# A two-block transformer kernel on one core: finer first tiles, an unsplit out-projection, and a reordered VectorE queue

## The reference, cut to what matters

```
mod = split(silu(c) @ ada_w + ada_b, 6)                  # ada_w: 1024 x 6144, one row vector c
a   = rmsnorm(x, g_pre) * (1 + mod[1]) + mod[0]
b_gate, c_gate, v = split(a @ sc_w_in, 3)                # 1024 x 3072
y   = (b_gate * depthwise_conv3(c_gate * v)) @ sc_w_out  # 1024 x 1024
x   = x + mod[2] * rmsnorm(y, g_post)
h   = rmsnorm(x, g_pre_ff) * (1 + mod[4]) + mod[3]
x   = x + mod[5] * rmsnorm(relu(h @ mlp_w_in)**2 @ mlp_w_out, g_post_ff)
```

## Time and profile before

| what | us |
|---|---|
| runs | 793.24 median of three (791.18 to 793.31) |
| profiled execution, its time | 792.01 |
| its span, first to last instruction | 790.2 |
| PE busy | 754.2 (95%) |
| DVE busy | 554.6 (70%) |
| ACT busy | 370.2 (47%) |
| moved by DMA | 152.17 MB, 193 GB/s |

### The profile page before, as it was taken

How to read it: one execution, slowest core, us unless ns; L and a number is a source line. 1 busy time by engine, 2 the same in 40 slices (tenths; PEclk the granted TensorE clock), 3 DMA queues, 4 the chain that set the end, 5 groups by cost and what they waited for, 6 DMA issues and landing times.

```text
span 790.2 us, 13306 instructions
## 1 busy us (share of the span) xinstructions
PE 754.2 (95%) x5388; PEld 709.3 (90%) x5388; DVE 554.6 (70%) x774; ACT 370.2 (47%) x463; POOL 10.7 (1%) x27
## 2 busy tenths in 40 slices
PE   4999979799999999999999999899998999999998
PEld 3789968699999888889988999899998999999998
DVE  4869887485656753466889977658757888887441
ACT  4124451465455333275555544673536555544330
POOL 0000000000000000020000000000000000000000
PEclk9899997799999999999999999999999999999999
DMA  9999795245456896435444244336652454533640
GB/s 317 349 376 333 241 362 216 107 160 194 180 171 200 282 303 196 177 120 213 160 160 160 107 161 147 109 119 213 213 213 107 160 196 177 183 123 121 209 138 27
DMA packets 52927, 152.17 MB, mean 193 GB/s; under 512 B 2640, under 2 KB 33488, under 8 KB 42512
## 3 DMA queue, kind: packets, MB, share of 16 engines
q1 hardware_dynamic: 52512, 150.20, 54.7%
q0 software_dynamic: 368, 1.31, 0.5%
HBM read 150.45 MB, written 1.05 MB: 192 GB/s over the span
## 4 chain that ended last, share of the span: by engine, by line
PE 75%; DVE 13%; ACT 4%; DMA 3%; issue 2%; SPq 2%; DVEq 0%; ACTq 0%
PE ps L1347 17%; PE ps L1349 17%; PE ps L1348 17%; PE ps L1471 5%; PE ps L1472 5%; PE ps L1473 5%; DVE w_lo L862 4%; DVE ada_acc L866 2%; DMA raw<-in_ada 2%; DVE cacc L1176 2%; ACT w_hi L493 1%; PE ps L1405 1%; DMA raw<-in_w_sc_in 1%; PE ps L1364 1%; PE ps L1489 1%
## 5 line engine op out<-in xcount | busy, mean ns | idle before, releaser
L862 DVE TENSOR_TENSOR w_lo<-raw,w_hi 128x2048 fp32r<-128x2048 f32 (+2 forms) x120 | 255.2, 2129 | 97.7 <-ACT w_hi L493 97.7
L1347 PE MATMUL ps<-a_hi,w_hi 128*128 128x256 f32 x1072 | 304.8, 284 | 0.8 <-DVE w_lo L862 0.7
L1349 PE MATMUL ps<-a_hi,w_lo 128*128 128x256 f32 x1072 | 302.9, 283 | 0.0
L1348 PE MATMUL ps<-a_lo,w_hi 128*128 128x256 f32 x1072 | 301.6, 281 | 0.0
L493 ACT ACTIVATE w_hi<-raw 128x2048 fp32r<-128x2048 f32 (+2 forms) x120 | 213.4, 1782 | 115.7 <-PE ps L1349 50.4
L1347 PEld LDWEIGHTS ps<-a_hi,w_hi 128*128 128x128 f32 x1072 | 202.1, 189 | 2.7 <-issue 1.7
L1348 PEld LDWEIGHTS ps<-a_lo,w_hi 128*128 128x128 f32 x1072 | 202.5, 189 | 0.7 <-issue 0.5
L1349 PEld LDWEIGHTS ps<-a_hi,w_lo 128*128 128x128 f32 x1072 | 201.0, 187 | 0.0
L866 DVE SCALAR_TENSOR_TENSOR ada_acc<-raw,silu_c,ada_acc 128x256 f32<-128x256 f32 (+1 forms) x77 | 53.5, 702 | 2.7
L1347 PE MATMUL ps<-up_hi,w_hi 128*128 128x256 f32 x176 | 49.9, 284 | 1.2 <-DVE up_lo L949 1.2
L1471 PE MATMUL ps<-w_hi,hid_hi 128*128 128x512 f32 x128 | 50.9, 398 | 0.0
(11 more groups left out here) (230 smaller groups left out, 915.3 us busy)
## 6 DMA issues: line engine op xcount, KB each, us to landing
raw<-in_w_z_in SPq DMA_DIRECT2D x26, 1024.0 KB, 4.8
raw<-in_w_up SPq DMA_DIRECT2D x22, 1024.0 KB, 4.7
raw<-in_w_mlp_in SPq DMA_DIRECT2D x16, 1024.0 KB, 4.9
raw<-in_w_mlp_out SPq DMA_DIRECT2D x16, 1024.0 KB, 5.7
raw<-in_w_down SPq DMA_DIRECT2D x16, 704.0 KB, 4.1
raw<-in_ada SPq DMA_DIRECT2D x16, 512.0 KB, 9.0
raw<-in_ada_half SPq DMA_DIRECT2D x8, 1024.0 KB, 6.6
raw<-in_ada SPq DMA_DIRECT2D x8, 1024.0 KB, 5.1
```

What stands on the lines that cost most here:

```text
L862: e.tensor_tensor(w_lo[:, slot, 0:words], raw[:, unit_slot, 0:words], w_hi[:, slot, 0:words].bitcast(f32), SUB).then_inc(raw_used, 1)
L1347: e.matmul(dst, w_hi[:, slot, cols], hi, start=start, stop=False, skip_group_check=skip)
L1348: e.matmul(dst, w_hi[:, slot, cols], lo, start=False, stop=False, skip_group_check=skip)
L1349: return e.matmul(dst, w_lo[:, slot, cols], hi, start=False, stop=stop, skip_group_check=skip)
```

## The change

1. The first stage goes by single feature tiles: part(t) loads 128 columns of scale and of shift (four DMAs of 256 KB in rows of 512 B, where there were rows of 1 KB), DVE sums both in one row of instructions (`tile_sum`), and PE's partition sums for tile k+1 stand after the third of four groups of tile k. For the first tile PE takes half of the shift's sum itself. The keys come in halves, x in two halves.
2. The norm of x is taken on features: ACT and DVE square, PE sums with ones, ACT takes the root. The turn of x to tokens moves behind (four tiles up front, four inside tiles 4 to 7).
3. The out-projection uses plain float32 products on weights that lie in their own tile `sc_w`, loaded once; no split of its weights or of `sc_y`.
4. DVE's order: the low part of the activations and of the first weights stands right behind the norm; convolution groups stand ahead of the half units, which become one instruction of 2048 columns each. The four units of mod[3] move behind the convolutions; the sums of mod[4] and mod[3] on PE move behind the first turn.

```diff
-HALVES_AHEAD = {2: 5, 5: 1, 6: 1, 7: 1}
-ADA_UNITS = {10: 1, 11: 3, 32: 1, 33: 1, 34: 1, 35: 1}
+RING = [("block", 0), ("block", 1), ("block", 2), ("block", 3), ("half", 0), ("block", 4), ("block", 5), ("half", 1),
+        ("block", 6), ("block", 7)] + [("half", i) for i in range(2, 8)] + [("block", 8), ("block", 9)] +        [("shift", i) for i in range(4)] + [("block", 10)]
+OUT_AT = {3: 0, 4: 1, 6: 2, 7: 3}
...
+            def part(t):
+                if t >= RAW_SLOTS:
+                    e.wait_ge(raw_used, t - RAW_SLOTS + 1)
                 for v in range(2):
-                    part(q, v)
+                    landed = first_shift_in if t == 0 and v else part_in[t]
+                    for i in range(2):
+                        at = (2 * v + i) * 512
+                        e.dma_start(raw[:, t % RAW_SLOTS, at:at + 512].rearrange("p (j f) -> p j f", j=4),
+                                    ada[4 * v:4 * v + 4].rearrange("j p (i f) -> i p j f", i=2)[i][:, :, t * P:(t + 1) * P])\
+                         .then_inc(landed, 16)
...
+            part(0)
+            keys(0, 0)
+            part(1)
+            keys(0, 1)
+            for q in range(1, 4):
+                part(2 * q)
+                part(2 * q + 1)
+                keys(q, 0)
+                keys(q, 1)
...
+            for t in range(DT):
+                modulated(t)
+                a_high(t)
+                if t == 6:
+                    x_by_token(2)
+                    high_at(0)
+            x_by_token(3)
...
+            def tile_sum(t):
+
+                e.wait_ge(part_in[t], 64)
+                e.wait_ge(raw_used, t)
+                acc = tile_acc[:, t % 2, :, :]
+                src = raw[:, t % RAW_SLOTS, :].rearrange("p (v i j f) -> p v i j f", v=2, i=2, j=4)
+                ch.link(e.tensor_scalar(acc, src[:, :, 0, 0, :], silu_c[:, 0:1], None, MUL))
                 for k in range(1, DT - 1):
-                    ch.link(ada_part(src(k), silu_c[:, k:k + 1], acc))
-                ada_part(src(DT - 1), silu_c[:, DT - 1:DT], acc).then_inc(raw_used, 1)
+                    ch.link(ada_part(src[:, :, k % 2, k // 2, :], silu_c[:, k:k + 1], acc))
+                ada_part(src[:, :, 1, 3, :], silu_c[:, 7:8], acc).then_inc(raw_used, 1)
...
             e.wait_ge(c_ready, 1)
-            part(0, 0)
-            part(0, 1)
-            scale_x(0)
+            first_tile(0, part_in[0], range(DT))
+            first_tile(1, first_shift_in, range(4, DT))
+            e.wait_ge(x_r, 1)
+            scale_x(0, 2)
             columns(0)
...
+            scale_x(2, DT)
+            for t in range(1, DT):
+                tile_sum(t)
+                columns(t)
+            e.wait_ge(act_hi, DT)
+            e.tensor_tensor(flat(a_lo[:, :, :]), flat(y[:, :, :]), flat(a_hi[:, :, :]).bitcast(f32), SUB).then_inc(act_lo, DT)
             low(0, 0, WORDS["sc_in"])
             low(1, 1, WORDS["sc_in"])
-            half_unit(0)
-            columns(3)
-            half_unit(1)
...
-                    if grp == 2 and k % 2 == 1 and k < DT - 1:
-                        part_sums(k // 2 + 1)
+                    if k % 2 == 0 and grp % 2 == 0:
+                        e.wait_ge(key_in[k // 2][grp // 2], 16)
                     mm = by_key(k, grp)
...
+                    if grp == 1 and k >= 4:
+                        turn_x(k)
+                    if grp == 2 and k < DT - 1:
+                        tile_columns(k + 1)
...
                     for k in range(DT):
-                        e.wait_ge(sc_ready, k + 1)
-                        mm = token_part(c, h, sc_hi[:, k, :], sc_lo[:, k, :], all_hi[:, 4 * h:4 * h + 4, k, :],
-                                        all_lo[:, 4 * h:4 * h + 4, k, :], k == 0, k == DT - 1)
...
+                        mm = e.matmul(ps[:, 2 * c + h, :].rearrange("p (n q) -> p n q", n=4), sc_y[:, k, c * P:(c + 1) * P],
+                                      by_feature[:, 4 * h:4 * h + 4, k, :], start=k == 0, stop=k == DT - 1)
+                    mm.then_inc(tok_done, 1)
                     if (c, h) == (0, 0):
-                        mod_sums(2, ada_acc[:, 2, :])
-                        mod_sums(4, ada_acc[:, 3, :])
+                        e.wait_ge(raw_used, ring_unit("half", 7) + 1)
+                        mod_sums(2, ada_acc[:, 0, :], MISC)
...
+            e.wait_ge(mod_read, 1)
+            e.wait_ge(gain_in, 2)
+            turn("post", 0, x_t)
+            e.wait_ge(raw_used, ring_unit("shift", 3) + 1)
+            mod_sums(4, ada_acc[:, 1, :], 1)
+            mod_sums(3, ada_acc[:, 2, :], 1)
             turn("post", 1, x_t)
```

More of the change, by code:

```diff
@@ L79, with ring_unit @@
 CV_MEAN_STEP, CV_VAR_STEP = 21, 22
+def ring_unit(kind, number):
+    return PARTS + RING.index((kind, number))
 def raw_unit(block):
-    return PARTS + block + sum(n for b, n in HALVES_AHEAD.items() if b <= block) + sum(b < block for b in ADA_OF)
-HALF_UNIT = [raw_unit(b) - n + i for b, n in HALVES_AHEAD.items() for i in range(n)]
+    if block < 11:
+        return ring_unit("block", block)
+    return PARTS + len(RING) + block - 11 + sum(b < block for b in VEC5_AFTER)
 class Chain:
@@ L229, in build_program @@
         par_in = sem("par_in")
-        x_landed = sem("x_landed")
+        x_landed = [sem(f"x_landed{h}") for h in range(2)]
         z_const_in = sem("z_const_in")
@@ L645, in _ @@
             high_at(3)
-            sc_high(0)
             sc_centre(1)
@@ L1112, in _ @@
-            ahead_at(g0 + 3)
+            half_unit(7)
+            g0 = FIRST["mlp_in"]
             mods(0, 2)
             e.tensor_tensor(gain_post[:, :], mod[:, 16:24], pcol("gains", 8, 8), MUL).then_inc(gain_cols, 1)
-            mods(1, 4)
-            ch.mark(e.scalar_tensor_tensor(gain_pre_ff[:, :], mod[:, 32:40], 1.0, pcol("gains", 16, 8), ADD, MUL))
+            ahead_at(g0)
+            ahead_at(g0 + 1)
+            for i in range(2):
+                ada_unit(ring_unit("shift", i), 2 * i, ada_acc[:, 2, :])
@@ L1117, in _, with rest_of_shift @@
             gain_evict(gain_b, 0)
-            e.wait_ge(x_tok_in, 4)
-            token_chain("post", 0, gain_b, x_tok, x_t)
-            mods(2, 3)
-            ahead_at(g0 + 4)
-            ahead_at(g0 + 5)
-            token_chain("post", 1, gain_b, x_tok, x_t)
+            e.wait_ge(x_tok_in, 3)
+            def rest_of_shift():
+                for i in range(2, 4):
+                    ada_unit(ring_unit("shift", i), 2 * i, ada_acc[:, 2, :])
+            token_chain("post", 0, gain_b, x_tok, x_t, rest_of_shift)
@@ L1124, in _, with scale_and_shift @@
+            def scale_and_shift():
+                mods(1, 4)
+                ch.mark(e.scalar_tensor_tensor(gain_pre_ff[:, :], mod[:, 32:40], 1.0, pcol("gains", 16, 8), ADD, MUL))
+                mods(2, 3)
+            token_chain("post", 1, gain_b, x_tok, x_t, scale_and_shift)
+            ch.wait()
             for i in range(DT):
```

434 lines of the change are left out of this document (201 added, 233 removed).

## The result

The changed kernel takes **786.08 us** (median of four, 785.41 to 786.78) against 793.04 us of the kernel before, measured beside it: a ratio of 0.992 [0.990, 0.993], 7.0 us or 0.9% faster. The forecast was 782 with a range of 775 to 790: right in direction and range, but it promised 10.9 us of gain where 7.0 came. The profiled execution took 785.41 us with a span of 783.9, against 792.01 and 790.2.

A forecast was written before the change was run, and what follows sets the result against it. PE, busy 95% of the span, was taken as the bound, the gain being how much earlier it reaches mlp_in: 3.1 (first stage) + 7.8 (up to the last turn) = 10.9 off 792.0, 781.1, or 782 on the median; range 775 to 790.

The forecast's parts named there:

- The start: First stage, up to by_key's first product: it comes at 15.2 us, 5.7 us earlier than before.
- The length: First stage, from by_key's first product: 51.8 us together, so the second stage starts at 67.0 instead of 70.15, 3.1 earlier.
- half clock's charge of 2.9: First stage: the half clock again lasts until 5.9 us behind the first product and costs 2.9 us.
- What hides under it: First stage: DVE's tiles covered by 1.2 us or more; loads at 293 GB/s land the last keys 5 us early.
- the small rows make the loads the bound: Rival, first stage: 512 B rows cost as much as 1 KB rows, 15 us later, 797 us; chance 0.09.
- The second stage: PE's 96 tiles take 35.5 us; DVE, the fuller queue, ends half unit 7 at 43.6 from the stage's start.
- the 47 that the prediction names as a sign of being wrong: Second stage: DVE at half unit 7 later than 47 us after the stage's start would show the forecast wrong.
- The out-projection: Products at 0.87 us, 1.1 of waiting for DVE, half clock charged 2.4; last turn at 78.0 instead of 85.8, 7.8 earlier.
- The sum: Whole kernel: 3.1 + 7.8 = 10.9 us off the profiled 792.0, so 781.1; 782 on the median.
- Behind mlp_in's start every stretch should be as long as before, within 0.5 us: Sign for the rest of the kernel, from mlp_in on: stretch lengths unchanged within 0.5 us.
- The clock stays down: Rival, out-projection: half clock through a quarter and more, 4.6 us on top, 787 us; chance 0.15.
- The clock stays up: Rival: PE hardly idles, so the 2.4 us loss, slow last turn and some first-stage half clock go; 776 us; chance 0.12.

The follow-up runs named there:

- e7: Changed kernel with the turns of x for tiles 4 to 7 moved ahead of by_key's products: 787.38 us, ratio 0.994 to the kernel before.
- e1: Changed kernel with the four 1 MB loads of the out-projection's weights moved in SP's queue: 783.50 us, ratio 0.988 to the kernel before.
- e2: Changed kernel with ACT computing group 4's centre tap ahead of block 6's high part: 784.83 us, ratio 0.991 to the kernel before.
- e3: Changed kernel with DVE's last convolution group ahead of half units 5 and 6, PE's mod[2] sums behind two out-projection quarters, mods later: 778.18 us, ratio 0.983.
- e5: Changed kernel with five products nobody reads put on PE ahead of its wait for the last convolution group: 783.07 us, ratio 0.988.
- e6: Changed kernel with the first stage's modulation weights laid out for rows of 2 KB instead of 512 B: 786.08 us, ratio 0.991.

## Why the prediction was right, and where it was off

**The start.** Forecast 15.2 for the first product, measured 16.08. The terms as written add up to 14.95 (8.3 + 4.6 + 0.7 + 0.6 + 0.75), so the sum itself is 0.25 too late. The pitch of 0.38 held (seven in 2.68). What was off is the time from which data can feed the first tile, 9.69 instead of 8.3. It was the load: DVE was through with x at 9.31 and then waited 0.37 us, as its row shows. x's second half had landed at 7.8, where the forecast had all of x at 6.5.

**The length.** Forecast 51.8, measured 65.80 - 16.08 = 49.7. The half clock's charge of 2.9 held: the first nine products took 6.96 us (16.08 to 23.04) instead of nine times 0.444, 3.0 more. Too dear were three small terms. The row moves on by 0.36 for a tile's column sums (23.04 to 23.41), seven times 2.5 and not 3.3; by 0.44 for a tile's turn (44.53 to 44.97 in the trace), four times 1.8 and not 2.3; and the gap of 0.1 a tile, 0.7, was not there. The busy time of a last record overlaps what follows, and I had counted it whole. The stage's gain is 4.35, not 3.1.

**What hides under it.** Right, with its number: 309 GB/s on the whole, 290 where only parts load (forecast 293), and no wait of PE. I gave it a cover of 5 us. It was thinner: the last keys landed at 55.1, 2.1 ahead of their first product at 57.25, and the half before them at 52.9, 1.3 ahead of its own at 54.15. And e7 shows that parts and block 0, not only the keys, are needed by a set time. The rival "the small rows make the loads the bound" did not happen, yet it stood one step behind: it decided as soon as PE got faster. The Trainium skill's "DMA: Bandwidth & Descriptors", section Specifications, gives 512 B as the smallest transfer for line rate. The trace disagrees for these loads: with rows of 512 B the stretch from 8 to 46 us ran at 309 GB/s, and at 290 where only they loaded; with rows of 2 KB it ran at 368, at the same DMA size of 256 KB. That comparison also answers the Trainium skill's rule of 1 MiB that the prediction weighed: it was the row, not the DMA, that was too small.

**The second stage.** PE's length was right (35.4 against 35.5). DVE's was the step that failed: "DVE ends half unit 7 at 43.6, and the last group one half unit earlier". Counted from the stage's start, it ended at 48.6, past the 47 that the prediction names as a sign of being wrong. The sum of DVE's work was right; 4.04 us of waiting for block 6's load were not in it, and about 0.8 for ACT in other groups beyond the 0.6 allowed. I had gone through the loads of the first stage and not through those of the second, where the change puts the 4 MB of the out-projection's weights into SP's queue among the blocks. e1 and e2 show the load as the cause.

**The out-projection.** A plain product costs 0.87, as forecast (32 records, 16 products, in 13.90). "Then it waits for half unit 7 until 43.6" became 4.85 + 0.19 us of waiting. The half clock I charged with 2.4. From start to start the sums took 3.44 instead of e3's 1.70, and the quarter 8.57 instead of 6.95: 3.4 in all. The one product ahead of them lost another 0.95 (2.07 instead of the 1.12 of e5), but under DVE's half unit 7, so it cost nothing. The norm chain of the second half was hidden as said, and the wait ahead of the last turn 0.86. In all the last turn came at 82.4 instead of 78.0: 5.0 for DVE, 0.8 more from half unit 7 to the first turn (1.0 for the clock, the small steps a little less than priced), and 1.3 less from the first turn to the last.

**The sum.** At mlp_in 7.9 us instead of 10.9. The two stretches erred in opposite directions, 4.35 instead of 3.1 up to the second stage and 3.4 instead of 7.8 from there to the last turn, and that kept the total nearer to the forecast than its main step deserved. "Behind mlp_in's start every stretch should be as long as before, within 0.5 us" was wrong in the profiled pair by 1.6: the half clock at 588, which the profiled execution of before happened not to have. A forecast counted from one execution carries that execution's luck with the clock.

**The rivals.** "The clock stays down" names 787, closer to the 786 measured than the forecast's 782, but that is luck: the clock brought 1.0 of its 4.6 us there, while the 5.0 us of DVE's lateness were not in it. "The clock stays up" came about by hand and in part, in e3: its sums and the quarter behind them ran at full speed, the first products and the last turn (3.53) did not.

## What to carry to other kernels

When a change adds loads, follow each queue's order on to the next transfer that somebody waits for: here three loads of 1 MB without a deadline, issued ahead of one block with one, made DVE wait 4.04 us. Where an engine is late, first ask what independent work the waiting engine has further back in its own queue; a new order of steps on the two engines (e3) gave 7.9 us, mending the lateness itself 1 to 3. A gain early in the kernel can be lost again to the half clock further on: in the profiles of e1 and e6 nothing of 2.1 and 1.0 us was left at mlp_in. And where two limits lie close together, each single edit looks as if it made no difference: take both away before dropping either.
